# The state-space mixer of a two-block network: gate operands split beside its outputs, second input table loaded by powers, third input product ahead of the first output half

## The chip, the cores and the metric

One core of one Trainium2 chip runs the whole program in one launch. The metric is the device time of one execution in microseconds (us); the median of three runs stands for a kernel. A fourth execution was recorded by the hardware profiler, and all durations below come from that one.

## The reference, cut to what matters

Two networks of depth 2 run one after the other on a sequence of 256 tokens of width 2048. The change touches one mixer, in the second layer of the second network: a state-space layer ("S5") with 128 groups of 16 channels and 64 complex states, cut into chunks of 64 tokens, followed by a gated linear unit:

```python
bu = einsum('bcgi,gpi->bcgp', u_c, b_bar)          # input product
_, states = associative_scan(combine, (a_elem, bu)) # scan along time
y = einsum('bcgp,gip->bcgi', states, c_mat).real    # output product
y = y + d_skip * u
z = gelu(y)
out = z * sigmoid(z @ w_glu + b_glu)                # gate product
```

Before it stands `u = rmsnorm(x) @ odd_w_in`, behind it `out @ odd_w_out`, and then cross-attention and a feed-forward block.

## The kernel before, in words

**Weight products.** Every dense product is a list of tiles ("pieces") of 128 output columns. A tile needs two halves of its weights, a rounded one and the remainder, split from a slab that a DMA brings into a ring of three slabs: ACT rounds all 16 row blocks (L306), DVE makes the remainder of the first eight (L322), POOL that of the last eight (L340). TensorE then runs 16 pairs of matmuls, the pair of L369 (512 columns, both halves of the operand) and L370 (256 columns). The operand itself is also split in two, by ACT (L427, `act_part`) and DVE (L432, `dve_part`), into `opa`, one block of 256 tokens for each of 16 row blocks. The split weights have two buffers in turn, so tile n+2 can be split only when tile n is done. PE, ACT, DVE, POOL and SP each have one instruction list in program order, with semaphore waits; an instruction that waits holds up everything behind it on its engine.

**The mixer.** `pe_odin` makes the 16 tiles of `u` (`K.U`, one row of it per tile). Then the 16 steps n of the scan, four to a stage s (s = 0 to 3), pass through the engines:
- `pe_s5_in(s)` is the input product of four steps, 128 calls of matmul and 256 instructions (L3583), 32 rows by 128 columns of weights from the table `TB[s % 2]` against 64 columns of U. The four row groups of the array take turns, q = 0 to 3. Its results `z5` go to four PSUM banks. The time index r runs over the four powers of the table, power 3 - r being 1024 columns of it.
- `dve_s5` has a body for every n: two products with the rotation table `tab` (L3657, L3664), two additions (L3674, L3675) into step n, and for the step before it the scan (L3671) and the product that makes `p` (L3682), and for the one before that `x` (L3661). ACT copies the scanned state for POOL (`w`, L3638) and makes the tables `tab` (L3545 to L3554), and POOL makes the other half of `p` and `x` (L3712, L3715).
- `pe_s5_out(s, h)` is one half of an output product: 48 instructions of a direct part (L3605) and 128 (L3614) on the p and x of the stage's four steps. `dve_s5_out` (L3697) adds the skip, u5, two rows for each half.
- After all of that ACT applies the gelu to the 16 rows (L3630), then ACT and DVE split them into `opa` (`act_glu`, `dve_glu`), and `pe_glu` runs the gate product: its tile 0 starts at L369 as soon as row block 0 is split.

**The order around the change is written out by hand.** `pe_s5` at L3557 issues in(1); then out(0,0), in(2), out(0,1), out(1,0), in(3), out(1,1), out(2,0), out(2,1), out(3,0), out(3,1). DVE puts the u5 of rows 0, 1 behind step 7, 2, 3 behind step 10, 4, 5 behind 11, 6, 7 behind 14, 8, 9 behind 15, the rest behind step 17. The banks set waits: in(2) may start only when `p` and `w` of step 4 are there, in(3) when those of step 8 are. All output halves but the last use one bank, so each waits for the u5 of the one before. `p5`, eight buffers, lies in a lent ring slab (four) and in the first half of `opa` (four). The p of steps 8 to 11 waits for out(0,1), that of steps 12 to 15 for out(1,1).

**Tables.** `sp_s5_tables` (L3414 on), on SP's queue, loads in this order: TB of stage 1 once tile 14 of `u` is done (`TB[1]` and `TC[1]` lie over the two weight buffers), the c table of stage 1 after tile 15, TB of stage 2 after in(0), the c table of stage 2 after out(0,1), TB of stage 3 after in(1), the c table of stage 3 after out(1,1). TB is loaded by two DMAs (512 KB and 1536 KB, L3375 and L3376), and a c table by one (L3367). The ring slabs lent to the scan are loaded again once the last output half is done.

Of the kernel before, what the change touches and what calls it, by code (L numbers as in the profile page):

```python
# [92 lines left out]
class K:  # L93


    def __init__(self, nc, ctx, D, at, cat):
# [1450 lines left out]
def places2(K):  # L1547
# [2019 lines left out]
def pe_s5_in(K, s):  # L3567

    pe = K.pe
    pe.wait_ge(*K.load[LOADED_B[s]].of(("tb", s)))  # L3570
    pe.wait_ge(*K.dve.of(("u", 4 * s + 3)))
    bs = K.z5b[4 * s:4 * s + 4]
    K.bank.update({("z5", 4 * s + q): bs[q] for q in range(4)})
    if s >= 2:
# [3 lines left out]
    for r in range(4):
        for m in range(4):
            for c in range(2):  # L3580
                for q in range(4):
                    q0 = 32 * q
                    t = pe.do.matmul(bs[q][:, 256 * c + 64 * m:256 * c + 64 * m + 64], B[q0:q0 + 32, 3 - r, m, c, :],  # L3583
                                     K.U[q0:q0 + 32, 4 * s + m, 64 * r:64 * r + 64], start=r + m + c == 0, stop=r + m + c == 7)
# [503 lines left out]
```

## Time and profile before

| what | value |
|---|---|
| median of 3 runs | 4016.72 us (4015.99, 4016.72, 4022.0) |
| profiled execution, own time | 4011.95 us |
| its span in the trace | 4010.6 us |
| mean granted TensorE clock | 0.979 of 2.4 GHz |
| PE busy | 94% of the span |
| DVE, ACT, POOL busy | 64%, 45%, 37% |
| mixer, start of in(1) to start of the gate product's tile 0 | 2867.21 to 2964.36 us |

The page cuts the span in 40 slices of about 100 us. PE is at 90% or more in most of them, and the slice that holds the mixer is one of the few at 80% with a granted clock of 0.8. A row of a timeline gives the start, the duration, the engine, the line, the operation and tiles, and in brackets how long the engine sat idle before it and what ended that. The granted clock is 1.00 at 2.4 GHz and 0.50 at 1.2 GHz.

### The profile page before, as it was taken

Reading aid. Unit: us, or ns where it says so; the run is one execution under the profiler, and the core shown is the slowest. Engines: PE = TensorE matmul, PEld = TensorE weight load, DVE = VectorE, ACT = ScalarE, POOL = GpSimd, SP = SyncE. Lnnn points to the kernel's source line nnn. Section 1 sums busy time; section 2 is a strip of 40 time slices with the busy share of each in tenths; the row PEclk is TensorE's granted clock in tenths of the full one; section 3 lists DMA queues with packets and bytes.
Section 4 is the critical chain, followed back from the end, with each engine's and each line's share of the span. In section 5 each row is a group of like instructions: output and inputs, shape, how many; then the busy total and the mean of one; then the engine's idle time right before and its main releaser. Section 6 shows DMA issues by size and latency. Waiting matters only on the chain.

```text
span 4010.6 us, 64383 instructions
## 1 busy us (share of the span) xinstructions
PE 3781.6 (94%) x27340; PEld 3219.0 (80%) x27340; DVE 2579.5 (64%) x3636; ACT 1799.7 (45%) x2801; POOL 1487.2 (37%) x726
## 2 busy tenths in 40 slices
PE   6898999998998999989999999999879999999998
PEld 3786888787877887888778888888768878888887
DVE  0435743786358897668879676876656776445457
ACT  1435443644345444445544444444445554333334
POOL 0332343233322441004344444444644434444443
PEclk8999999999999999999999999999889999999999
DMA  9653665454643453005355564656445435455553
GB/s 388 271 231 147 235 258 200 161 190 167 247 171 121 171 185 122 23 8 227 139 179 221 199 242 183 227 226 255 162 151 207 168 130 194 181 191 187 189 188 127
DMA packets 60655, 748.64 MB, mean 187 GB/s; under 512 B 6976, under 2 KB 9152, under 8 KB 16720
## 3 DMA queue, kind: packets, MB, share of 16 engines
q1 hardware_dynamic: 48960, 696.74, 45.8%
q0 software_dynamic: 9344, 45.69, 3.0%
q8 instruction: 216, 3.54, 0.4%
q10 hardware_dynamic: 2064, 2.10, 0.1%
q14 instruction: 71, 0.58, 0.0%
HBM read 727.65 MB, written 16.84 MB: 186 GB/s over the span
## 4 chain that ended last, share of the span: by engine, by line
PE 75%; DVE 15%; ACT 5%; DMA 2%; issue 1%; POOL 1%; another core or an unknown queue 0%; SPq 0%; DVEq 0%; ACTq 0%; POOLq 0%
PE ps L369 42%; PE ps L370 21%; DVE pieces L322 3%; DMA ring<-in_ada 2%; ACT pieces L306 2%; PE ps L2228 2%; PE ps L789 2%; DVE opb L570 1%; DVE r L1172 1%; PE ps L3583 1%; DVE opa L570 1%; PE ps L1898 1%; DVE scr L527 1%; DVE scr L591 1%; PE ps L643 1%
## 5 line engine op out<-in xcount | busy, mean ns | idle before, releaser
L369 PE MATMUL ps<-opa,pieces 128*128 128x512 f32 x6192 | 2248.9, 406 | 60.0 <-DVE pieces L322 36.0
L340 POOL TENSOR_TENSOR pieces<-ring,pieces 128x1024 fp32r<-128x1024 f32 x539 | 1348.1, 2501 | 2181.9 <-ACT pieces L306 2163.3
L370 PE MATMUL ps<-opa,pieces 128*128 128x256 f32 x6192 | 1740.6, 281 | 0.0
L306 ACT ACTIVATE pieces<-ring 128x1024 fp32r<-128x1024 f32 (+1 forms) x1110 | 1098.5, 1036 | 807.7 <-PE ps L370 807.0
L369 PEld LDWEIGHTS ps<-opa,pieces 128*128 128x128 f32 x6192 | 1170.9, 189 | 352.6 <-issue 40.1
L370 PEld LDWEIGHTS ps<-opa,pieces 128*128 128x128 f32 x6192 | 1177.7, 190 | 8.9 <-issue 5.3
L369 PE MATMUL ps<-opb,pieces 128*128 128x512 f32 x2560 | 909.1, 396 | 19.4 <-DVE pieces L322 13.7
L322 DVE TENSOR_TENSOR pieces<-ring,pieces 128x1024 fp32r<-128x1024 f32 (+1 forms) x571 | 728.4, 1276 | 269.1 <-ACT pieces L306 265.6
L370 PE MATMUL ps<-opb,pieces 128*128 128x256 f32 x2560 | 725.3, 283 | 0.0
L369 PEld LDWEIGHTS ps<-opb,pieces 128*128 128x128 f32 x2560 | 482.8, 189 | 141.2 <-issue 15.3
L370 PEld LDWEIGHTS ps<-opb,pieces 128*128 128x128 f32 x2560 | 483.4, 189 | 0.1
L427 ACT ACTIVATE opb<-scr 128x256 fp32r<-128x256 f32 x129 | 53.9, 418 | 451.3 <-DVE scr L3072 450.8
L381 DVE TENSOR_REDUCE scr<-ps 128x256 f32<-128x512 f32 x203 | 139.8, 689 | 162.0 <-PE ps L370 161.6
L408 DVE TENSOR_TENSOR x<-ps,x 128x256 f32<-128x256 f32 x192 | 80.8, 421 | 192.5 <-PE ps L370 192.4
L789 PE MATMUL ps<-ring,ada 128*32 128x256 f32 x1536 | 104.5, 418 | 38.1 <-DMA ring<-in_ada 38.1
L527 DVE TENSOR_TENSOR scr<-scr 128x256 f32<-128x256 f32 x165 | 126.3, 783 | 14.5 <-ACT scr L518 11.3
L591 DVE TENSOR_TENSOR scr<-scr,rstd 128x256 f32<-128x256 f32 x136 | 131.1, 964 | 4.6
L789 PEld LDWEIGHTS ps<-ring,ada 128*32 128x32 f32 x1536 | 48.7, 117 | 78.6 <-DMA ring<-in_ada 28.8
L381 DVE TENSOR_REDUCE m<-ps 128x256 f32<-128x512 f32 x48 | 33.2, 691 | 112.1 <-PE ps L370 112.1
L432 DVE TENSOR_TENSOR opb<-scr,opb 128x256 fp32r<-128x256 f32 x129 | 54.8, 425 | 62.5 <-ACT opb L427 62.5
L832 ACT ACTIVATE scr<-ps 128x256 f32<-128x256 f32 x48 | 18.4, 384 | 166.9 <-PE ps L803 148.1
L1063 ACT ACTIVATE scr<-m 128x256 f32<-128x256 f32 x48 | 20.0, 418 | 161.9 <-DVE m L381 161.8
(432 smaller groups left out, 3308.9 us busy)
## 6 DMA issues: line engine op xcount, KB each, us to landing
ring<-in_up SPq DMA_DIRECT2D x64, 2048.0 KB, 7.8
ring<-in_down SPq DMA_DIRECT2D x64, 2048.0 KB, 7.8
ring<-in_win SPq DMA_DIRECT2D x56, 2048.0 KB, 7.6
ring<-in_ada SPq DMA_DIRECT2D x48, 2048.0 KB, 11.9
ring<-in_wout SPq DMA_DIRECT2D x24, 2048.0 KB, 7.6
ring<-in_evin SPq DMA_DIRECT2D x18, 2048.0 KB, 7.8
ring<-in_evout SPq DMA_DIRECT2D x8, 2048.0 KB, 7.8
ring<-in_xkv SPq DMA_DIRECT2D x8, 2048.0 KB, 7.8
```

The source lines that it names most:

```text
L306: a.do.activation(K.parts_of(p)[0][:, s, :], w[:, s, :], ACT.Copy).then_inc(*K.hi.up((p, h)))
L322: v.do.tensor_tensor(lo[:, s, :], w[:, s, :], hi[:, s, :].bitcast(F), ALU.subtract).then_inc(*K.lo.up(p))
L340: g.do.tensor_tensor(lo[:, s, :], w[:, s, :], hi[:, s, :].bitcast(F), ALU.subtract).then_inc(*K.lo2.up(p))
L369: pe.do.matmul(b[:, 0:512], hi[:, k, :], op[:, 512 * k:512 * k + 512], start=i == 0, stop=False)
L370: t = pe.do.matmul(b[:, 0:256], lo[:, k, :], half(op, 0, k), start=False, stop=i == kt - 1)
L381: return K.v.do.tensor_reduce(out, b, AX.X, ALU.add)
L408: v.do.tensor_tensor(x, b[:, 0:256], x, ALU.add).then_inc(*K.dve.up())
L527: v.do.tensor_tensor(K.acc[z], K.acc[z], K.sqr[z][k % 2], ALU.add).then_inc(*K.dve.up((*key, "acc", k)))
L570: K.v.do.scalar_tensor_tensor(out=half(op, 1, k), in0=src, scalar=gain, in1=half(op, 0, k).bitcast(F), op0=ALU.mult, op1=ALU.subtract).the ...
L591: return v.do.tensor_tensor(out, out, rstd[0:out.shape[0]], ALU.mult)
L789: t = pe.do.matmul(b[q:q + 32, 0:256], K.sc[:, 2 * k:2 * k + 32], w[:, k, :], start=k < 4, stop=k >= 12)
L2228: t = K.pe.do.matmul(b[r, 64 * i:64 * i + 64], w[r, i, :], x[r, i, :] if len(x.shape) == 3 else x[r, :], start=start, stop=stop)
```

## The change

The input product of stage 2 moves in front of the first output half, and that of stage 3 in front of out(1,0). The table of stages 1 and 3 is loaded in four DMAs of 512 KB, each with a semaphore of its own, in the order in which the product reads them. The product of stage 1 no longer waits for the last row of u as a whole: the three row groups whose banks are free come first. More output halves have banks of their own. The u5 steps move, the gelu and the first operand splits are put between the last steps, and the p buffers move to the second half of `opa`.

```diff
-    K.p5 = rot(rb, 0, 4, 1024) + rot(f, 8192, 4, 1024)
+    K.p5 = rot(rb, 0, 4, 1024) + rot(f, 12288, 4, 1024)
...
+def load_powers(K, e, s):
+    for k in range(3, -1, -1):
+        src = K.D["s5tb"][s][:, 1024 * k - 1024:1024 * k] if k else K.D["s5b"][s]
+        e.do.dma_start(K.TB[1][:, 1024 * k:1024 * k + 1024], src).then_inc(*K.load["pw%d" % k].up(("tb", s, k), 16))
...
-    load_b(K, sp, 1)
+    load_powers(K, sp, 1)
...
     sp.wait_ge(*K.prod.of(("y5", 3)))
     load_c(K, sp, 2)
     sp.wait_ge(*K.prod.of(("z5", 7)))
-    load_b(K, sp, 3)
+    load_powers(K, sp, 3)
...
 def pe_s5(K):
-    K.pe.wait_ge(*K.dve.of(("u", 15)))
     pe_s5_in(K, 1)
-    for s in range(4):
+    pe_s5_in(K, 2)
+    pe_s5_out(K, 0, 0)
+    pe_s5_out(K, 0, 1)
+    pe_s5_in(K, 3)
+    for s in range(1, 4):
         pe_s5_out(K, s, 0)
-        if s < 2:
-            pe_s5_in(K, s + 2)
         pe_s5_out(K, s, 1)
...
+    rounds = [((0, 1), (0, 1, 2)), ((0, 1), (3,)), ((2, 3), (0, 1, 2, 3))] if s == 1 else [((0, 1, 2, 3), (0, 1, 2, 3))]
+    for powers, rows in rounds:
+        if s == 1 and 3 in rows:
+            pe.wait_ge(*K.dve.of(("u", 15)))
+        for r in powers:
+            if s % 2:
+                pe.wait_ge(*K.load["pw%d" % (3 - r)].of(("tb", s, 3 - r)))
...
+Y5_AT = {(1, 1): 5, (2, 1): 6, (3, 1): 5}
+Y5_AFTER = {(0, 1): 1, (1, 0): 3, (2, 0): 5, (3, 0): 9, (3, 1): 7}
...
+    pe.wait_ge(*K.act.of(("w", {(1, 1): 9, (2, 1): 10}.get((s, h), 0))))
+    if (s, h) in Y5_AFTER:
+        pe.wait_ge(*K.dve.of(("u5", Y5_AFTER[s, h])))
...
-    for n in (13, 14, 15):
-        act_s5_rows(K, n)
-    for i in range(16):
-        a.wait_ge(*K.dve.of(("u5", i)))
-        a.do.activation(K.U[:, i, :], K.U[:, i, :], ACT.Gelu_apprx_tanh).then_inc(*K.act.up(("gelu", i)))
+    a.wait_ge(*K.prod.of(("z5", 15)))
+    act_feed(K, K.first["glu"])
+    act_s5_rows(K, 13)
+    act_s5_gelu(K, 0, 4)
+    act_s5_rows(K, 14)
+    act_s5_gelu(K, 4, 8)
+    act_s5_parts(K, 0, 4)
+    act_s5_rows(K, 15)
+    act_s5_gelu(K, 8, 10)
+    act_s5_parts(K, 4, 8)
+    act_s5_gelu(K, 10, 14)
+    a.wait_ge(*K.prod.of(("y5", 15)))
+    act_s5_parts(K, 8, 14)
+    for i in (14, 15):
+        act_s5_gelu(K, i, i + 1)
+        act_s5_parts(K, i, i + 1)
...
+U5_BEHIND = {7: 0, 10: 2, 13: 4, 14: 6, 16: 8, 17: 10}
...
-    for i in range(10, 16):
+    dve_feed(K, K.first["glu"])
+    for i in range(8):
+        dve_part(K, K.opa, ("gl",), i, K.U[:, i, :])
+    for i in range(12, 16):
         dve_s5_out(K, i)
...
 def dve_glu(K):
     v, p = K.v, K.first["glu"]
-    v.wait_ge(*K.prod.of(("y5", 15)))
-    v.wait_ge(*K.act.of(("gelu", 15)))
-    dve_feed(K, p)
-    for i in range(16):
+    for i in range(8, 16):
         dve_part(K, K.opa, ("gl",), i, K.U[:, i, :])
```

`act_s5_gelu` and `act_s5_parts` are the old loops over gelu and `act_part`, cut to a range of rows. `U5_BEHIND[n]` names the first of the two rows of u5 put behind step n. U rows 12 to 15 stand behind the splits of rows 0 to 7. `Y5_AT` gives the bank and `Y5_AFTER` the row of u5 that an output half waits for. The first six lines of `act_glu` (feed and 16 splits) are gone.

## Rows read from the trace of the kernel before

**Rows 1.** Timeline of PE: start, duration, engine, line, operation, count, idle before.

```profile
2839.82 7.37 PE L3583 MATMUL ps<-s5u 32*128 32x64 f32 x256
...
2867.21 11.90 PE L3583 MATMUL ps<-s5u,s 32*128 32x64 f32 x256 [2.54 <-DVE ps L3671]
...
2886.32 3.60 PE L3614 MATMUL ps<-ring,mix 128*32 128x63 f32 x128 [4.49 <-DVE ps L3674]
...
2897.18 1.51 PE L3605 MATMUL ps<-s5u,scr 32*32 32x192 f32 x48
2898.63 1.97 PE L3614 MATMUL ps<-ring,mix 128*32 128x63 f32 x128
2910.10 2.78 PE L3605 MATMUL ps<-s5u,scr 32*32 32x192 f32 x48 [9.50 <-DVE s5u L3697]
...
2915.24 8.01 PE L3583 MATMUL ps<-s5u,s 32*128 32x64 f32 x256
...
2957.72 0.32 PE L3614 MATMUL ps<-s 128*32 128x64 f32 x7 [1.61 <-issue]
2964.36 0.76 PE L369 MATMUL ps<-opa,pieces 128*128 128x512 f32 x1 [6.32 <-DVE opa L432]
```

**Rows 2.** Timeline of DVE, same columns.

```profile
2879.17 0.69 DVE L3657 TENSOR_TENSOR ring<-ps,ring 128x512 f32<-128x512 f32 x1 [2.83 <-PE ps L3583]
...
2895.04 0.86 DVE L3697 SCALAR_TENSOR_TENSOR s5u<-s5u,cols,ps 128x256 f32<-128x256 f32 x2
2897.33 0.69 DVE L3657 TENSOR_TENSOR ring<-ps,ring 128x512 f32<-128x512 f32 x1 [1.42 <-PE ps L3583]
...
2923.30 0.69 DVE L3657 TENSOR_TENSOR ring<-ps,ring 128x512 f32<-128x512 f32 x1 [7.07 <-PE ps L3583]
...
2944.82 0.69 DVE L3682 TENSOR_TENSOR s<-ps,s5u 128x512 f32<-128x512 f32 x1
...
2961.65 7.59 DVE L432 TENSOR_TENSOR opa<-s5u,opa 128x256 fp32r<-128x256 f32 x16
...
2972.07 0.69 DVE L381 TENSOR_REDUCE mix<-ps 128x256 f32<-128x512 f32 x1 [1.70 <-PE ps L370]
...
2977.62 0.69 DVE L381 TENSOR_REDUCE mix<-ps 128x256 f32<-128x512 f32 x1 [2.04 <-PE ps L370]
```

**Rows 3.** Timeline of ACT: the end of table 4, and the copy w of step 4.

```profile
2876.50 0.40 ACT L3554 ACTIVATE ring<-scr 128x256 f32<-128x256 f32 x1
...
2887.27 0.60 ACT L3638 ACTIVATE scr<-ps 128x512 f32<-128x512 f32 x1 [1.24 <-DVE s L3682]
```

**Rows 4.** Windows: PE, PEld, DVE, ACT, POOL busy (x instructions), granted clock, DMA, GB/s.

```profile
2867.20:2879.10 11.90, 11.89 (x260) 11.78 (x264) 9.13 (x20) 8.07 (x21) 9.25 (x8) 0.60 0.77 325
...
2886.30:2889.90 3.60, 3.58 (x132) 3.43 (x132) 3.60 (x9) 2.57 (x8) 3.02 (x3) 0.50 0.02 5
...
2900.60:2910.10 9.50, 0.00 (x1) 0.01 (x1) 9.50 (x21) 6.41 (x16) 7.99 (x7) 0.66 0.89 347
...
2915.30:2923.20 7.90, 7.85 (x260) 7.56 (x259) 0.87 (x2) 2.71 (x8) 4.76 (x4) 1.00 0.02 4
```

**Rows 5.** DMA issues from 2858 to 2880 us: tiles, size, us to landing.

```profile
s<-in_s5b SPq DMA_DIRECT2D x1, 512.0 KB, 3.2
```

**Rows 6.** DMA issues from 2900 to 2916 us, all behind the end of out(0,1).

```profile
s<-s_b_tables SPq DMA_DIRECT2D x1, 1536.0 KB, 11.9
s<-in_s5b SPq DMA_DIRECT2D x1, 512.0 KB, 8.7
```

**Rows 7.** Line L3583: its instructions, duration in ns min/median/max.

```profile
L3583 PEld LDWEIGHTS ps<-s5u x512: 181/187/217, 2839.8 to 2896.9; 32*128 32x128 f32 x171
L3583 PE MATMUL ps<-s5u x512: 270/270/354, 2839.8 to 2897.0; 32*128 32x64 f32 x171
```

**Rows 8.** Timeline of POOL: the split of the last eight blocks of tile 0.

```profile
2961.48 2.45 POOL L340 TENSOR_TENSOR pieces<-ring,pieces 128x1024 fp32r<-128x1024 f32 x1 [13.15 <-ACT pieces L306]
```

**Rows 9.** DMA issues from 2957 to 2985 us.

```profile
ring<-in_glu SPq DMA_DIRECT2D x4, 2048.0 KB, 7.8
```

More of the change, by code:

```diff
@@ L3569, in pe_s5_in @@
     pe = K.pe
-    pe.wait_ge(*K.load[LOADED_B[s]].of(("tb", s)))
-    pe.wait_ge(*K.dve.of(("u", 4 * s + 3)))
     bs = K.z5b[4 * s:4 * s + 4]
     K.bank.update({("z5", 4 * s + q): bs[q] for q in range(4)})
+    pe.wait_ge(*K.dve.of(("u", 4 * s + 3) if s == 0 else ("u", 14)))
     if s >= 2:
@@ L3576, in pe_s5_in @@
         pe.wait_ge(*K.act.of(("w", 4 * s - 4)))
+    if s % 2 == 0:
+        pe.wait_ge(*K.load["tb%d" % s].of(("tb", s)))
     B = K.TB[s % 2].rearrange("p (k m c t) -> p k m c t", k=4, m=4, c=2)
[L3578 to L3584, printed above, removed]
+    rounds = [((0, 1), (0, 1, 2)), ((0, 1), (3,)), ((2, 3), (0, 1, 2, 3))] if s == 1 else [((0, 1, 2, 3), (0, 1, 2, 3))]
[5 more added lines that the diff above has]
+                pe.wait_ge(*K.load["pw%d" % (3 - r)].of(("tb", s, 3 - r)))
+            for m in range(4):
+                for c in range(2):
+                    for q in rows:
+                        q0 = 32 * q
+                        t = pe.do.matmul(bs[q][:, 256 * c + 64 * m:256 * c + 64 * m + 64], B[q0:q0 + 32, 3 - r, m, c, :],
+                                         K.U[q0:q0 + 32, 4 * s + m, 64 * r:64 * r + 64], start=r + m + c == 0, stop=r + m + c == 7)
     t.then_inc(*K.prod.up(("z5", 4 * s + 3)))
+Y5_AT = {(1, 1): 5, (2, 1): 6, (3, 1): 5}
+Y5_AFTER = {(0, 1): 1, (1, 0): 3, (2, 0): 5, (3, 0): 9, (3, 1): 7}
 def pe_s5_out(K, s, h):
     pe = K.pe
-    b = K.bank["y5", s, h] = K.ps[5] if (s, h) == (3, 1) else K.ps[3]
+    b = K.bank["y5", s, h] = K.ps[Y5_AT.get((s, h), 3)]
     pe.wait_ge(*K.act.of(("K", 0)))
-    pe.wait_ge(*K.act.of(("w", 12 if (s, h) == (3, 1) else 0)))
-    if s + h and (s, h) != (3, 1):
-        pe.wait_ge(*K.dve.of(("u5", 4 * s + 2 * h - 1)))
+    pe.wait_ge(*K.act.of(("w", {(1, 1): 9, (2, 1): 10}.get((s, h), 0))))
+    if (s, h) in Y5_AFTER:
+        pe.wait_ge(*K.dve.of(("u5", Y5_AFTER[s, h])))
     if s:
@@ L3625, in act_s5, with act_s5_gelu, act_s5_parts @@
             act_s5_whole(K, n // 2 + 1)
-    for n in (13, 14, 15):
-        act_s5_rows(K, n)
-    for i in range(16):
-        a.wait_ge(*K.dve.of(("u5", i)))
-        a.do.activation(K.U[:, i, :], K.U[:, i, :], ACT.Gelu_apprx_tanh).then_inc(*K.act.up(("gelu", i)))
+    a.wait_ge(*K.prod.of(("z5", 15)))
[14 more added lines that the diff above has]
+        act_s5_parts(K, i, i + 1)
+def act_s5_gelu(K, i, j):
+    for i in range(i, j):
+        K.a.wait_ge(*K.dve.of(("u5", i)))
+        K.a.do.activation(K.U[:, i, :], K.U[:, i, :], ACT.Gelu_apprx_tanh).then_inc(*K.act.up(("gelu", i)))
+def act_s5_parts(K, i, j):
+    K.a.wait_ge(*K.tile.of(K.first["odin"] + 15))
+    for i in range(i, j):
+        K.a.wait_ge(*K.act.of(("gelu", i)))
+        act_part(K, K.opa, ("gl",), i, K.U[:, i, :])
 def act_s5_rows(K, n):
```

24 lines of the change are left out of this document (7 added, 17 removed).

## The prediction

> **What bounds the kernel now.** The page comes first: PE is busy nearly everywhere, so only the places where it stands still can give something back, and the slice with the mixer is one of them. Then the timelines of PE and DVE side by side. In the mixer the two hand the work to and fro. PE stands 4.49 us before the second part of out(0,0) and 9.50 us before out(1,0); DVE starts step 4 only with the end of in(1), after 2.83 us idle, step 8 with the end of in(2) after 1.42, and step 12 with the end of in(3) after 7.07 [rows 1, 2]. Then comes the tail: the last output half ends at 2958.04, and PE waits 6.32 us until a first row of `opa` is split, at 2964.36; tile 0 is done at 2972.07 [rows 1, 2]. So what counts is which of the four input products DVE waits for, and the tail. Last the windows, for TensorE's clock: it is at 1.00 in the one product in(3) and at 0.60 over in(1) [rows 4].
>
> From the end of tile 0 on nothing is changed and PE is the bound (tiles end 5.55 us apart, at 2972.07 and 2977.62 [rows 2]), so the shift of that end is the shift of the whole. I follow the change from in(1) to it, in times of the old trace.
>
> **in(1).** Its last table quarter came with a whole 1536 KB load; now the first quarter is 512 KB, and such a load alone took 3.2 us [rows 5], so it is there before tile 15 ends (about 2864.7, 2.54 us before 2867.21 [rows 1]). The product starts at 2864.7 without a pause. Its rounds: 96 instructions on three row groups, 32 on one, 128 on four. The normal spacing is 7.37/256 = 0.029 us [rows 1]. For the 32 on one row group there is no row. Bounds: 0.029 each (0.9 us), or load and matmul one after the other, 187 + 270 = 457 ns [rows 7], 14.6 us. I take 0.06 (1.9 us), twice the spacing of the nearest row, which is in(0) [rows 1], since weight load and matmul of different instructions plainly overlap there. Sum 2.8 + 1.9 + 3.7 = 8.4, end 2873.1; with the high value 2885.8. DVE needs it for step 4, but also `tab` of step 4, whose last instruction ends at 2876.90 [rows 3] and hangs on POOL's angles, which don't move. So step 4 starts at 2876.9, 2.3 us earlier, and in(1) has 3.8 us to spare, up to 0.18 us for each of the 32. By the Trainium skill, "TensorE: Matmul & The Clock Gate", section Part 3, a weight load overlaps running matmuls only when its row group differs. By that rule the loads of the single group alone, 32 x 187 ns, would take 6.0 us, in(1) would end at 2877.2, and step 4 would lose 0.3 us; no row here shows such a round. Four DMA issues for two on SP's queue cost some 0.9 us of its time, hidden: what is queued behind them (c table 1, table 2) is wanted only after 2885.
>
> **in(2), moved ahead.** It waits for w of step 4. That ended 8.70 us after step 4 began (2887.87 less 2879.17 [rows 2, 3]); so now at 2885.6. PE has then stood since 2873. At which clock does it run? In the old trace the clock is down after pauses (0.50 with out(0,0) after 4.49 us idle, 0.66 over 9.5 us of nothing [rows 1, 4]), and in(1) itself ran 11.9 us at a mean of 0.60 without coming back: 7.37/0.60 = 12.3, so these 32-row matmuls did not lift it, while the 128-row matmuls of L3614 did (0.50 at 2886.3, then in(2) at full speed in front of L3605's 1.51 us) [rows 1, 4]. in(3) ran in 8.01 at 1.00 because it followed out(1,0). So I take a cold in(2): twice the 7.37 less what is fixed, 14.0 us, against 7.4 warm. It ends at 2899.6, and the old one ended at 2897.18 [rows 1].
>
> **out(0,0), now behind it, and who waits.** Direct part cold 2.78, L3614 between 1.97 and 3.60, say 2.8 [rows 1]: it ends at 2905.2. In DVE's list u5 of rows 0, 1 stands behind step 7 and in front of step 8, and needs this half. DVE is through step 7 at 2892.8 (its end moved by 2.3 from 2895.04 [rows 2]) and stands 12.4 us. After 0.86 for u5 [rows 2] step 8 starts at 2906.1: **8.8 us later** than 2897.33.
>
> **Steps 8 to 11, out(0,1), in(3).** out(0,1) runs warm 1.51 + 1.97 less overlap = 3.4, ends 2909.5. SP has the c table of stage 2 in front of the quarters, and both behind this end: the first 512 KB after such an end landed 8.7 us after an issue 0.4 us behind it, the rest of the table 11.9 after its own [rows 6]. So in(3) starts at about 2918.6, after 9 us idle, cold, 14.0 us, end 2932.6. DVE would be ready at 2906.1 + 4 x 3.97 + 0.8 = 2922.8 (a step is (2895.04 - 2879.17)/4 = 3.97 [rows 2]), so in(3) decides again. Step 12 starts **9.3 us later** than 2923.30.
>
> **Steps 12 to 17.** out(1,0) 5.6 (2.78 + 2.8) to 2938.2, out(1,1), in its own bank, 3.4 to 2941.6. The p of step 12, due at 2939.9, waits for it: 1.7 us lost. Then u5 of 4, 5, steps 14 and 15 with u5 of 6, 7 to 2951.8, step 16 without its products 2.4 (to 2954.2), u5 of 8, 9 to 2955.0. Here out(2,0) and out(2,1) lie beside the steps. out(3,0), waiting for that u5, starts 2955.0 at the low clock, 5.6, and out(3,1) 3.4: end at **2964.0**. Old: from step 12 at 2923.30 to 2958.04 34.7 us, new 31.4, so 3.3 saved, since DVE no longer feeds the halves one by one. The old p of step 15 came at 2944.82 [rows 2], and then PE worked off three halves.
>
> **The tail.** Gelu, tile 0's split by ACT and DVE, and the splits of rows 0 to 7 lie beside steps 14 to 17 and out(3,0). The split of eight rows on DVE costs at most 7.59/2 = 3.8 us [rows 2]; behind 2955.8 it is over at 2961, before y of out(3,0) is wanted by u5 of 12, 13. If that cover is gone it costs these 3.8. At 2964.0 PE starts tile 0 at once, warm. POOL's remainder for blocks 8 to 15 needs 2.45 [rows 8], PE comes to block 8 after 2.8 us, half of 5.55. The eight late rows on DVE come 0.41 apart and tile 0 takes them at 0.35, which adds 0.2. End of tile 0 at 2969.8: 5.8 us behind the last half where it was 14.0, **8.2 saved**. The next slab is issued with the end of out(3,1) and lands 7.8 later [rows 9], 2971.8; with 2.3 us of splits 2974.1, tile 2 is due at 2975.4: hidden, with 1.3 to spare.
>
> **Sum.** +9.3 - 3.3 - 8.2 = -2.2 us. Profiled execution 4011.95 - 2.2 = 4009.8; the median of the runs is 4.8 above that execution, so 4016.72 - 2.2 = **4014.5 us**. A difference of 0.2% (8 us) is about what a measurement can tell from none.
>
> **Rivals.**
> - *B, in(2) is warm.* Then 7.4 us, end 2893.0, out(0,0) 3.5, step 8 at 2897.4, as before; in(3) still late by its table and cold, step 12 at 2923.9. Sum +0.6 - 3.3 - 8.2 = -10.9: 4005.8. For it: in(0) and in(3) ran at full clock. Against it: 9.8 us of cold in(1) with no rise. The Trainium skill ("TensorE: Matmul & The Clock Gate", Part 1) has the clock released by sustained activity, which would lift in(2) in its course; in(1)'s row speaks against it for this form. Chance 0.2, with mixtures.
> - *C, the single row group.* From 0.18 us for each of the 32, in(1) becomes late. At 0.457 and a low clock in its last round (7.0) it ends at 2889, 12 us behind 2876.9, and steps 4 on with it: -2.2 + 12 = +10: 4026.5. For it: nothing in the trace runs on one row group alone with so few columns. Against: the tight spacing of in(0), 0.029 us where a load lasts 0.187 [rows 1, 7]. Chance 0.08.
> - *D, the cover in the tail fails*: the eight early splits stand in front of the last u5, PE waits their 3.8 us, and the stall of 1.61 us on issue before the last seven matmuls [rows 1] returns. -2.2 + 3.8 + 1.6 = +3.2: 4019.9. Chance 0.12.
> - *E, the change doesn't do what it says*: the two moved products save no wait, since DVE stands for out(0,0) and in(3) for its table, and the splits are waited for as before. Then the losses of 9.3 stand against 3.3 alone: +6, 4022.7. The wait on `opa` is gone by the code, so I give it no chance of its own; it is in C's.
>
> **How the numbers follow.** The forecast has 0.6, with a range of its own of 4009.5 to 4019 (each of three clock changes may fall 1.5 us earlier or later). To hold 8 in 10 the range goes down to B, 4005, and up to D, 4020.5. Faster by over 0.2% is B: 0.2. Slower by over 0.2% is C and a little of D: 0.1. Same 0.7.
>
> **What would show it.** Right: L3583 starts at 2864.7 with no idle time; DVE's L3697 for rows 0 and 1 has over 10 us idle before it, released by L3614; in(2) lasts near 14 us at 0.5; in(3) starts 9 us behind the end of out(0,1); PE's idle time before the first L369 of the gate product is gone. Wrong: step 8 of DVE starts before 2900, or in(2) lasts under 9 us (B); step 4 starts after 2878 (C); a pause over 2 us before tile 0 (D).

## The result and the profile after

The changed kernel runs in 4018.88 us (median of 20 runs, 4016.77 to 4027.71), the kernel before in 4014.89 us (20 runs, 4005.71 to 4026.82). The ratio is 1.0014, with a 95% interval of 1.0007 to 1.0020: **5.6 us slower**, 2.8 to 8.0 (the medians alone are 4.0 apart). Forecast were 2.2 us less; 4018.88 lies inside the range given, but the sign is the other one. The profiled execution of the changed kernel took 4020.42 us (span 4019.1, mean granted clock 0.978) where that of before took 4011.95, so the two traces differ by 8.5 us. Of these, 1.3 us lie ahead of the mixer: tile 15 of u ends at 2865.94 and not at 2864.67.

The timeline of PE after the change (start, duration, engine, line, operation, tiles, count, idle before and its releaser; L3594 is the old L3583, L3620 the old L3605, L3629 the old L3614):

```profile
2865.66 0.28 PE L370 MATMUL ps<-opa,pieces 128*128 128x256 f32 x1
2865.87 15.27 PE L3594 MATMUL ps<-s5u,s 32*128 32x64 f32 x256
2889.96 13.93 PE L3594 MATMUL ps<-s5u 32*128 32x64 f32 x256 [8.82 <-DVE ring L3701]
2903.82 2.78 PE L3620 MATMUL ps<-s5u,scr 32*32 32x192 f32 x48
2906.53 2.96 PE L3629 MATMUL ps<-ring,mix 128*32 128x63 f32 x128
...
2923.20 13.93 PE L3594 MATMUL ps<-s5u,s 32*128 32x64 f32 x256 [9.28 <-DVE s5u L3741]
...
2954.80 1.18 PE L3620 MATMUL ps<-s5u,scr 32*32 32x128 f32 x38 [3.47 <-issue]
...
2963.73 1.97 PE L3629 MATMUL ps<-s 128*32 128x63 f32 x128 [2.02 <-POOL s L3759]
...
2967.79 0.31 PE L3620 MATMUL ps<-s5u,scr 32*32 32x64 f32 x7 [0.72 <-issue]
...
2971.26 0.32 PE L3629 MATMUL ps<-s 128*32 128x64 f32 x7 [1.33 <-issue]
2971.51 0.50 PE L369 MATMUL ps<-opa,pieces 128*128 128x512 f32 x1
```

Against [rows 1]: in(1) starts without a pause, but lasts 15.27 us where the old one took 11.90 and the forecast was 8.4. in(2) and in(3) are both 13.93 us long, where the old trace had 7.4 and 8.01. A product that runs at 1.2 GHz is called cold below, one at 2.4 GHz warm. in(3) itself waits for no u5 (L3741) in the program; run 11 has the load of its table at this place, and run 7 tests it. In the last line the gate product follows the last output half at once; the 6.32 us of waiting in [rows 1] are gone.

The timeline of DVE, same columns (L3701 is the old L3657, L3741 the old L3697):

```profile
2881.18 0.69 DVE L3701 TENSOR_TENSOR ring<-ps,ring 128x512 f32<-128x512 f32 x1 [3.57 <-PE ps L3594]
...
2909.57 0.87 DVE L3741 SCALAR_TENSOR_TENSOR s5u<-s5u,cols,ps 128x256 f32<-128x256 f32 x2 [12.45 <-PE ps L3629]
2910.36 0.68 DVE L3701 TENSOR_TENSOR ring<-ps,ring 128x512 f32<-128x512 f32 x1
...
2937.18 0.69 DVE L3701 TENSOR_TENSOR ring<-ps,ring 128x512 f32<-128x512 f32 x1 [9.36 <-PE ps L3594]
...
2962.93 3.29 DVE L432 TENSOR_TENSOR opa<-s5u,opa 128x256 fp32r<-128x256 f32 x8
...
2977.78 0.67 DVE L381 TENSOR_REDUCE mix<-ps 128x256 f32<-128x512 f32 x1
```

The four L3701 and L3741 rows are the starts of step 4, of u5 for rows 0 and 1, and of steps 8 and 12. The 12.45 us in front of u5 are the stand that was forecast (12.4). The last row starts 0.20 us behind the end of tile 0 on PE (2977.58), from which the times below are taken.

The windows of the same trace (us, then PE, PEld, DVE, ACT, POOL busy (x instructions), granted clock, DMA share, GB/s):

```profile
2869.40:2870.90 1.50, 1.50 (x24) 1.50 (x21) 1.50 (x4) 1.15 (x3) 0.47 (x1) 1.00 1.07 459
2870.90:2889.90 19.00, 10.24 (x146) 10.05 (x145) 15.43 (x32) 11.12 (x30) 15.66 (x14) 0.51 0.36 149
2889.90:2903.80 13.90, 13.84 (x256) 13.77 (x256) 7.22 (x15) 8.34 (x22) 12.81 (x11) 0.50 0.01 3
2903.80:2908.50 4.70, 4.70 (x128) 3.92 (x128) 0.00 (x0) 0.00 (x0) 0.00 (x0) 0.50 0.00 0
```

The clock falls at 2871.1, inside in(1), and is at its lower level for 37.5 us, through all of in(2) and most of out(0,0). In the third row PE is busy the whole time and the clock doesn't move.

Step by step, in us behind the end of tile 15 of each trace:

| point | before | forecast | after | after less forecast |
|---|---|---|---|---|
| in(1) ends | 14.4 | 8.4 | 15.2 | +6.8 |
| step 4 starts | 14.5 | 12.2 | 15.2 | +3.0 |
| in(2) | 25.2 to 32.6 | 20.9 to 34.9 | 24.0 to 37.9 | +3.0 |
| step 8 starts | 32.7 | 41.4 | 44.4 | +3.0 |
| in(3) | 50.6 to 58.6 | 53.9 to 67.9 | 57.3 to 71.2 | +3.3 |
| out(3,0) starts | 83.3 | 90.3 | 94.3 | +4.0 |
| last half ends | 93.4 | 99.3 | 105.6 | +6.3 |
| tile 0 ends | 107.4 | 105.1 | 111.6 | +6.5 |
| tile 15 ends | 190.6 | | 197.0 | |

So the miss at tile 0 is 3.0 us from in(1), 0.3 on the way to in(3), 3.0 within the output halves and 0.2 behind them. The next 15 tiles add 2.2 us that the forecast had at nothing, and what comes behind tile 15 the last 0.7 of the 8.5.

### The profile page after: what moved, and what is told of

The parts are those of the page before. It is cut to its first block, busy times and chain, and to the rows that moved or that the text cites. A ratio compares the mean times of both kernels' runs of the same rounds, so it can differ in the third digit from the quotient of the medians.

```text
span 4019.1 us, 64388 instructions
## 1 busy us (share of the span) xinstructions
PE 3796.4 (94%) x27340; PEld 3230.7 (80%) x27340; DVE 2575.8 (64%) x3636; ACT 1798.9 (45%) x2801; POOL 1481.9 (37%) x726
## 4 chain that ended last, share of the span: by engine, by line
PE 77%; DVE 14%; ACT 5%; DMA 2%; issue 1%; POOL 1%; another core or an unknown queue 0%; SPq 0%; DVEq 0%; ACTq 0%; POOLq 0%
PE ps L369 43%; PE ps L370 22%; DVE pieces L322 2%; DMA ring<-in_ada 2%; ACT pieces L306 2%; PE ps L2228 2%; PE ps L789 2%; PE ps L3594 1%; DVE r L1172 1%; PE ps L1898 1%; DVE opa L570 1%; DVE scr L591 1%; PE ps L643 1%; PE ps L1043 1%; DVE opb L570 1%
## 5 line engine op out<-in xcount | busy, mean ns | idle before, releaser
L322 DVE TENSOR_TENSOR pieces<-ring,pieces 128x1024 fp32r<-128x1024 f32 (+1 forms) x571 | 721.5, 1264 | 268.5 <-ACT pieces L306 265.1
L369 PEld LDWEIGHTS ps<-opb,pieces 128*128 128x128 f32 x2560 | 482.7, 189 | 141.0 <-issue 15.3
L427 ACT ACTIVATE opb<-scr 128x256 fp32r<-128x256 f32 x129 | 53.9, 418 | 451.0 <-DVE scr L3072 450.5
L527 DVE TENSOR_TENSOR scr<-scr 128x256 f32<-128x256 f32 x165 | 126.2, 782 | 14.5 <-ACT scr L518 11.3
```

Source lines behind the costliest of these rows:

```text
L322: v.do.tensor_tensor(lo[:, s, :], w[:, s, :], hi[:, s, :].bitcast(F), ALU.subtract).then_inc(*K.lo.up(p))
L369: pe.do.matmul(b[:, 0:512], hi[:, k, :], op[:, 512 * k:512 * k + 512], start=i == 0, stop=False)
L527: v.do.tensor_tensor(K.acc[z], K.acc[z], K.sqr[z][k % 2], ALU.add).then_inc(*K.dve.up((*key, "acc", k)))
```

## The experiments

The letters in the expectations: **R**, the rounds of in(1) cost time; **O**, the place of in(2) does; **C**, the clock is what makes in(2) and in(3) long; **T**, step 12 hangs on in(3) and its table and not on step 8; **L**, the profile of before shows an execution with an early rise of the clock. "Tile 0" below is its end behind the end of tile 15 of u, as in the table.

**1. in(1) in one round.**

```diff
-    rounds = [((0, 1), (0, 1, 2)), ((0, 1), (3,)), ((2, 3), (0, 1, 2, 3))] if s == 1 else [((0, 1, 2, 3), (0, 1, 2, 3))]
+    rounds = [((0, 1, 2, 3), (0, 1, 2, 3))]
```

> The changed kernel with in(1) in one round of four row groups, power by power, waiting for the last row of u; all else kept. In the changed kernel in(1) took 15.27 us: 3.6 for the 96 on three row groups, 3.9 for the 32 on one, the rest at the low clock, and step 4 of DVE began 15.2 us behind the end of tile 15 (14.5 before the change). Theory R (the rounds are the loss): in(1) takes 8 to 13 us, step 4 begins 12.3 to 14 us behind tile 15, and all that follows moves with it, 1.5 to 3 us less for the kernel. Rival P (the quarters of the table arrive too late for any order): step 4 stays at 15 us or later, no gain.

Measured: ratio to before 1.0005 (0.9996 to 1.0014). in(1) 12.02 us, 3.2 less than with rounds, though it starts 1.5 later behind the last row of u; step 4 at 13.5 (15.2), tile 0 at 110.2 (111.6). The rounds cost 1.7 us at step 4, at the low end of R: in(1) in one round is still long, since the clock falls 2.1 us after its start all the same (0.58 mean). in(2) and in(3) stay at 13.93. The ratio was 1.0014 with the rounds, so 3.6 us less by the runs, which were measured at another time than those of the changed kernel.

**2. in(2) back behind out(0,0).**

```diff
-    pe_s5_in(K, 2)
     pe_s5_out(K, 0, 0)
+    pe_s5_in(K, 2)
```

> The changed kernel with in(2) put back behind out(0,0); in(3) stays ahead of out(1,0). Theory O (the order of in(2) is the loss: it runs at the low clock after a pause, and DVE stands for out(0,0) behind it): in(2) takes 7.4 us instead of 13.9, DVE's idle time of 12.45 us before u5 of rows 0 and 1 is gone, step 8 begins 34 to 35 us behind tile 15 instead of 44.4, and the kernel is 8 to 11 us faster than the changed one, so 3 to 6 us faster than the kernel before. Rival W (step 12 waits for the table of stage 3 and for the clock whatever happens before): step 8 gains 10 us, step 12 under 4 us, the kernel under 4 us.

Measured: 0.9996 (0.9985 to 1.0006). PE's timeline of this kernel:

```profile
2865.21 15.24 PE L3594 MATMUL ps<-s5u,s 32*128 32x64 f32 x256
...
2891.11 7.37 PE L3594 MATMUL ps<-s5u 32*128 32x64 f32 x256
...
2911.37 13.93 PE L3594 MATMUL ps<-s5u,s 32*128 32x64 f32 x256 [9.54 <-DVE s5u L3741]
```

in(1) is as long as in the changed kernel and in(2) is warm again. Step 8 starts at 33.3 (44.4), tile 0 ends at 100.8 (111.6). The sign is that of O, but not all of the 10.9 us belongs to the order. In this order in(2) was cold in two other traces (runs 3 and 9), and there step 8 starts at 39.9: at the same clock the place of in(2) is worth 4.5 us at step 8, and the other 6.6 are the clock. By the runs the kernel is 1.6 us faster than before (6.0 faster to 2.4 slower), where 3 to 6 were expected.

**3. The old order and loads, the new tail alone.** The moves of in(2) and in(3), the rounds and the loads by powers are undone; the u5 places, the banks, the gelu and the early splits stay.

```diff
-    for k in range(3, -1, -1):
...
+    e.do.dma_start(K.TB[1][:, 0:1024], K.D["s5b"][s]).then_inc(*K.load["pw0"].up(("tb", s, 0), 16))
+    e.do.dma_start(K.TB[1][:, 1024:4096], K.D["s5tb"][s]).then_inc(*K.load["pw1"].up(("tb", s, 1), 16))
...
-    pe_s5_in(K, 2)
-    pe_s5_out(K, 0, 0)
-    pe_s5_out(K, 0, 1)
-    pe_s5_in(K, 3)
-    for s in range(1, 4):
+    for s in range(4):
         pe_s5_out(K, s, 0)
+        if s < 2:
+            pe_s5_in(K, s + 2)
...
```

> Tail alone: the changed kernel with the order of products, the single round and the two-part table loads of before; what stays is the gelu and the splits between the steps, the u5 places, the banks and the place of the p buffers. Both products warm as before, steps 8 and 12 at 32.7 and 58.6 us behind tile 15 as before. Theory: the last half ends about 92 us behind tile 15 and tile 0 of the gate product 6 us after it, so 8 to 10 us less than before the change (0.2 to 0.25%). Rival S (the stalls on issue in the output halves, 7.3 us in the changed kernel against 3.0 before, belong to the tail part of the change): the last half ends at 95 or later, and the gain is 3 to 5 us.

Measured: 0.9989 (0.9980 to 0.9998), so 4.4 us faster where 8 to 10 were expected. In the profile tile 0 ends at 105.1, only 2.3 before that of the kernel before, although 6.0 us lie between the last half and tile 0 (14.0 before). The trace shows why: in(2) took 13.93 us here, in the very order in which the old timeline has it at 7.4. The row of this run, and that of the kernel before:

```profile
2891.68 13.93 PE L3592 MATMUL ps<-s5u 32*128 32x64 f32 x256
...
2889.86 7.40 PE L3583 MATMUL ps<-s5u 32*128 32x64 f32 x256
```

This run made L: two executions with the same instructions in this place are not in the same clock. Runs 9 and 10 test it.

**4. The clock held up in front of in(2).** 22 matmuls whose result nothing reads, on 128 rows and 512 columns; nothing else differs.

```diff
     pe_s5_in(K, 1)
+    K.pe.wait_ge(*K.act.of(("w", 0)))
+    for _ in range(22):
+        K.pe.do.matmul(K.ps[3][:, 0:512], K.opa[:, 0:128], K.opa[:, 0:512], start=True, stop=True)
     pe_s5_in(K, 2)
```

> The changed kernel with 22 extra matmuls of 128 rows by 512 columns, whose result nobody reads, between in(1) and in(2), in the pause of 8.82 us. Theory C (the cold in(2) is the clock's doing and not a property of the product): the granted clock is 1.00 when in(2) begins, in(2) takes 7.4 to 8.5 us instead of 13.93, out(0,0) 3.5 instead of 5.7, and step 8 begins 7 to 9 us earlier than in the changed kernel. Rival: in(2) takes over 12 us (32-row matmuls with no clock above the low one after a pause), no gain or a loss by what the extra work adds. For the kernel: the gain carries over to step 12 if the table of stage 3, ordered at the end of out(0,1), moves with it: 6 to 9 us less.

Measured: 1.0001 (0.9991 to 1.0012). PE's timeline, and the windows of all engines:

```profile
2866.10 15.92 PE L3597 MATMUL ps<-s5u,s 32*128 32x64 f32 x256
2881.95 7.95 PE L3564 MATMUL ps<-opa 128*128 128x512 f32 x22
2890.76 7.37 PE L3597 MATMUL ps<-s5u 32*128 32x64 f32 x256 [0.87 <-DVE ring L3704]
```

```profile
2884.00:2886.00 2.00, 2.00 (x7) 1.52 (x6) 2.00 (x5) 0.00 (x0) 0.45 (x1) 0.50 0.00 0
2886.00:2888.00 2.00, 2.00 (x7) 1.57 (x6) 2.00 (x5) 1.84 (x5) 1.20 (x1) 0.58 0.00 0
2888.00:2890.70 2.70, 1.89 (x9) 1.23 (x7) 2.70 (x7) 1.44 (x5) 2.17 (x3) 1.00 0.00 0
...
2890.70:2898.10 7.40, 7.33 (x260) 7.30 (x261) 7.23 (x15) 4.91 (x14) 6.65 (x6) 1.00 0.02 4
```

The clock rises while the added matmuls run, near 2888. At 1.00 in(2) takes 7.37 us; tile 0 ends at 105.1, 6.5 before that of the changed kernel. Order, rounds and waits are the changed kernel's, so the long in(2) is the clock's doing: C holds. in(3), with no such work in front, is cold again (14.23). Expected were 6 to 9 us less for the kernel than changed; the runs give 1.0001 beside 1.0014 of the changed kernel, so 5 less, again from runs at another time.

**5. The rounds in in(0) too**, one execution.

```diff
-    rounds = [((0, 1), (0, 1, 2)), ((0, 1), (3,)), ((2, 3), (0, 1, 2, 3))] if s == 1 else [((0, 1, 2, 3), (0, 1, 2, 3))]
+    rounds = [((0, 1), (0, 1, 2)), ((0, 1), (3,)), ((2, 3), (0, 1, 2, 3))] if s < 2 else [((0, 1, 2, 3), (0, 1, 2, 3))]
```

> The cost of the rounds by itself: the changed kernel with in(0), which runs in the middle of full-speed tiles, cut into the same three rounds as in(1). In the changed kernel in(0) takes 7.37 us. Inside in(1) the 96 on three row groups went 37 ns apart, the 32 on one at 112 ns while the clock was still full, then up to 175. Theory G (single row group: load and matmul of neighbours no longer overlap): in(0) takes 96 x 0.037 + 32 x 0.112 + 128 x 0.029 = 10.9 us at full clock. Rival K (the clock's fall made the round slow, not the row group): in(0) takes 7.4 to 8.5 us. Between the two lies the case that the clock falls during the round, then 12 to 15 us.

Measured: 4032.59 us in its one execution. in(0) stands amid the tiles of u, all its data there, at full clock. The timeline and the windows of this line alone:

```profile
2845.91 15.27 PE L3594 MATMUL ps<-s5u 32*128 32x64 f32 x256
```

```profile
2845.90:2849.40 3.50, 3.49 (x96) 3.49 (x99) 1.00 0.00 0
2849.40:2853.30 3.90, 3.90 (x38) 3.90 (x34) 0.73 0.02 4
2853.30:2861.00 7.70, 7.70 (x133) 7.69 (x133) 0.50 0.01 2
```

in(0) takes 15.27 us where [rows 1] has 7.37. The three windows are the three rounds. The starts of the single instructions in the trace show how they go. In each turn the matmuls of the different row groups start together, 6 to 7 ns apart, and the next turn follows 112 ns later at the full clock and 213 ns later at the low one, whether one, three or four groups take part. That is 112 ns for each instruction on one group, 37 on three and, in in(0) as it was, 29 on four; at the low clock 213 on one and 53.4 on four. So the instruction count is not the cost, but the turns: 96/3 + 32 + 128/4 = 96 of them in rounds, 64 in one round of four groups. In(1) of the changed kernel has the same paces, in its windows of this line:

```profile
2865.90:2869.40 3.50, 3.50 (x99) 3.50 (x100) 1.00 0.95 309
2869.40:2873.30 3.90, 3.90 (x40) 3.90 (x36) 0.72 0.99 417
2873.30:2880.80 7.50, 7.50 (x133) 7.50 (x132) 0.50 0.61 253
```

The round on one group takes 4.1 us for 32 instructions (from 2869.38 to 2873.47 in the changed kernel). In run 5 the clock comes down within it, 5.25 us after the start of in(0), with no wait and hardly a transfer about (DMA share 0.00 to 0.02); in the other 13 traces in(0) has no rounds and keeps 1.00 to its end. It is the case between the two theories (12 to 15 us): G's price for the rounds, 32 turns more, and the clock's fall on top. That the rounds bring the clock down is shown in this one execution alone, and for in(0) alone; in(1) loses it without rounds too (run 1).

**6. The u5 of rows 0, 1 behind step 8**, one execution.

```diff
-U5_BEHIND = {7: 0, 10: 2, 13: 4, 14: 6, 16: 8, 17: 10}
+U5_BEHIND = {8: 0, 10: 2, 13: 4, 14: 6, 16: 8, 17: 10}
```

> The changed kernel with u5 of rows 0 and 1 put behind step 8 instead of step 7, so that step 8 of DVE needs in(2) alone. Step 8 begins at 38 us behind tile 15 instead of 44.4. Theory T (in(3) waits for its table, which is loaded behind out(0,1), and step 12 for in(3)): out(0,1), the table, in(3) and step 12 stay where they are, 48, 57, 71 us, and the kernel gains nothing. Rival D (DVE's chain of steps sets the end): step 12 begins 4 to 6 us earlier and the kernel gains as much.

Measured: 4021.24 us. Step 8 starts at 40.3 (44.4), but in(3) at 59.2 (57.3) and step 12 at 73.2 (71.2): DVE's stand moves from u5 to step 12, where it idles 12.98 us. in(1) ended 1.6 us later in this execution, which is most of the 2.0 at step 12. T: nothing gained.

**7. The powers of stage 3 in front of the c table of stage 2**, one execution.

```diff
-    sp.wait_ge(*K.prod.of(("y5", 3)))
-    load_c(K, sp, 2)
     sp.wait_ge(*K.prod.of(("z5", 7)))
     load_powers(K, sp, 3)
+    sp.wait_ge(*K.prod.of(("y5", 3)))
+    load_c(K, sp, 2)
```

> The changed kernel with the quarters of the stage 3 table ordered ahead of the wait for out(0,1) and of the c table of stage 2. They land long before 45 us behind tile 15. in(3) then waits only for w of step 8, about 53 us, instead of 57.2 us. Theory T: in(3) begins 4 us earlier, at the low clock again (5 us pause), 13.9 us long, step 12 at 67 instead of 71.2, the last half and the gate product 4 us earlier. Rival (issue stalls and POOL's last x decide the end): step 12 gains 4 us, the gate product under 2.

Measured: 4011.03 us. in(3), in PE's timeline of this kernel:

```profile
2916.82 13.93 PE L3594 MATMUL ps<-s5u,s 32*128 32x64 f32 x256 [5.15 <-DVE ring L3701]
```

Its idle time falls from 9.28 to 5.15 us and its releaser is now DVE's step 8. Step 12 starts at 67.1 (71.2), tile 0 ends at 107.1 (111.6). T again: the table was what held in(3).

**8. All together:** one round, in(2) behind out(0,0), powers first, and in the tail ACT's tables of step 15 before the splits of rows 0 to 3 and DVE's weight split of the gate product behind its eight operand splits.

```diff
-    act_s5_parts(K, 0, 4)
     act_s5_rows(K, 15)
+    act_s5_parts(K, 0, 4)
...
-    dve_feed(K, K.first["glu"])
     for i in range(8):
         dve_part(K, K.opa, ("gl",), i, K.U[:, i, :])
+    dve_feed(K, K.first["glu"])
```

> All repairs together: in(1) in one round, in(2) behind out(0,0), the stage 3 quarters ahead of out(0,1), and in the tail ACT's copy of step 15 ahead of the splits of rows 0 to 3 and DVE's split of tile 0 behind the eight splits. Expected: step 4 at 13.5 us behind tile 15, step 8 at 31 to 35, in(3) begins at w of step 8, about 41, and lasts 8 (full clock) to 14 us, step 12 at 50 to 55 instead of 71, the last half at 84 to 89, tile 0 of the gate product ends at 90 to 95 where it ended at 107.4 before the change and 111.6 after. Kernel 12 to 17 us (0.3 to 0.4%) faster than before. Rival: stalls on issue in the output halves grow as PE has fewer pauses to fetch in, and half of it is lost.

Measured: 0.9975 (0.9964 to 0.9986), median 4003.48 us: 10 us faster than the kernel before, where 12 to 17 were expected. PE's timeline:

```profile
2871.81 7.36 PE L3594 MATMUL ps<-s5u,s 32*128 32x64 f32 x252 [1.46 <-DVE s5u L401]
2881.50 0.44 PE L3594 MATMUL ps<-s5u,s 32*128 32x64 f32 x4 [2.33 <-issue]
...
2951.66 1.97 PE L3629 MATMUL ps<-s 128*32 128x63 f32 x128 [0.93 <-POOL s L3759]
```

Step 8 starts at 32.2, step 12 at 55.1, the last half ends at 89.7, tile 0 at 95.7. The wait for POOL's x in the last halves is 0.93 us instead of 2.02. in(3) is still cold, 13.93 us. in(1), the same single round as in run 1, ran warm to its end here (7.36 us before its stall, 12.02 in run 1): its clock too differs from execution to execution.

**9. The kernel before, profiled again.**

> The kernel before, profiled once more, nothing changed. In its first profile in(1), in(2), in(3) took 11.9, 7.4 and 8.0 us, and DVE's steps 8 and 12 began 32.7 and 58.6 us behind the end of tile 15. Theory L (at which clock a product runs depends on where the clock's changes fall, which is another place in each execution): one or more of the three products has another length, by 1 to 6.5 us, and step 12 begins anywhere between 57 and 66. Rival (fixed by the program): the same lengths within 0.3 us.

Measured: 4028.94 us. PE's timeline of this second execution:

```profile
2874.61 12.54 PE L3583 MATMUL ps<-s5u,s 32*128 32x64 f32 x256 [2.49 <-DMA s<-s_b_tables]
...
2894.48 3.60 PE L3614 MATMUL ps<-ring,mix 128*32 128x63 f32 x128 [4.63 <-DVE ps L3674]
2898.01 13.93 PE L3583 MATMUL ps<-s5u 32*128 32x64 f32 x256
...
2931.82 7.37 PE L3583 MATMUL ps<-s5u,s 32*128 32x64 f32 x256 [0.41 <-DMA s<-s_b_tables]
```

```profile
2889.70:2898.00 8.30, 3.67 (x136) 3.39 (x128) 8.30 (x17) 5.15 (x14) 5.87 (x6) 0.71 0.01 2
2898.00:2911.90 13.90, 13.90 (x264) 13.77 (x260) 6.07 (x14) 6.48 (x17) 10.99 (x10) 0.50 0.01 3
```

The same code, and in(2) takes 13.93 us and not 7.4. The clock came back for a part of the first window and was down again before in(2); in [rows 4] it was up just ahead of it. Tile 0 ends at 117.2 and not at 107.4. L holds: the trace on which the forecast rests was the better of the two by 9.8 us in this stretch. But 4028.94 is also more than any of the 77 timed executions of this kernel (4005.06 to 4027.35), so this second trace is an extreme one and not the usual case.

**10. The new tail alone, once more, with more rounds.** The kernel of run 3.

> The tail alone, the kernel of e3_old_order once more. There in(2) took 13.93 us against 7.4 in the profile of before, though the work ahead of it is the same, and the gain at tile 0 was 2.3 us instead of 8 to 10. Theory L (that was the place of the clock's changes): with in(2) at full speed the last half ends at 92 to 94 and tile 0 at 98 to 100 us behind tile 15. If in(2) is cold again: 105 as in the first look. The timed runs average over it: 4 to 9 us faster than before.

Measured: 0.9967 (0.9955 to 0.9979), median 4004.12 us. Here in(2) took 7.53 us and tile 0 ended at 97.9. The four traces pair up: warm against warm, the tail saves 107.4 - 97.9 = 9.4 us, cold against cold 117.2 - 105.1 = 12.1. By the ratio it is 13.3 us, more than the 4 to 9 expected and three times the 4.4 of run 3, with the same kernel. The two went to different chips, their intervals just fail to meet, and the kernel before had a median of 4013.51 us beside run 3 and of 4017.22 beside run 10. So one ratio can be some 9 us off the next, beyond its own interval, and only kernels that were measured together are set side by side below.

**11. The changed kernel, profiled again.**

> The changed kernel, profiled once more. in(2) follows a pause of over 8 us and a stretch at the low clock: theory L says that it and in(3) are cold in each execution (13.9 us both), as in e1, e5, e6 and e7, so the changed kernel has lost a lottery that the kernel before wins at times; only in(1) may vary, 15 to 17 us. Tile 0 of the gate product ends 110 to 114 us behind tile 15. Rival: in(2) or in(3) under 12 us.

Measured: 4015.87 us. in(1) 15.38, in(2) and in(3) 13.93 each, step 12 at 71.3, tile 0 at 111.5: within 0.2 us of the first trace. In all six traces with in(2) in front of out(0,0) and no added matmuls (the two of the changed kernel, runs 1, 5, 6 and 7) in(2) and in(3) take 13.93 us; behind out(0,0) in(2) took 7.4 to 8.0 in five traces and 13.93 in two. In the changed kernel the slow clock is no matter of luck, and that fits the runs: before spreads over 21 us, after lies within 6 us in 19 of 20.

**12. Run 8 with the clock held up before in(1) and in(3)** by 6 and 22 such unread matmuls.

```diff
+def pe_busy(K, bank, n):
+    for _ in range(n):
+        K.pe.do.matmul(bank[:, 0:512], K.opa[:, 0:128], K.opa[:, 0:512], start=True, stop=True)
...
+    pe_busy(K, K.z5b[4], 6)
     pe_s5_in(K, 1)
...
+    K.pe.wait_ge(*K.dve.of(("p", 5)))
+    K.pe.wait_ge(*K.act.of(("w", 5)))
+    pe_busy(K, K.z5b[12], 22)
     pe_s5_in(K, 3)
```

> e8_all with extra matmuls of 128 rows by 512 columns that nobody reads: 6 in front of in(1) (pause 1.46 us) and 22 between out(0,1) and in(3) (pause 5.6 us). Theory C (the low clock behind a pause is what makes the products slow): in(1) takes 7.4 to 8 us in every execution, in(3) 7.4 to 8 us instead of 13.93, step 12 begins at 49 to 50 us behind tile 15 instead of 55, bound by DVE's own steps, and the kernel is 4 to 6 us faster than e8_all. Rival: in(3) is no faster, or step 12 begins at 54 or later since the extra matmuls hold it up; no gain.

Measured: 0.9950 (0.9937 to 0.9964), median 3998.52 us against 4017.22 of before and 4004.12 of run 10, measured together, with no overlap with the latter's runs (3996.50 to 4001.51; 4003.43 to 4008.56). It is the **best version** here. PE's timeline:

```profile
2870.20 1.55 PE L3562 MATMUL ps<-opa 128*128 128x512 f32 x6
2871.84 7.14 PE L3603 MATMUL ps<-s5u,s 32*128 32x64 f32 x246
2880.23 0.55 PE L3603 MATMUL ps<-s5u,s 32*128 32x64 f32 x10 [1.25 <-issue]
2894.58 7.58 PE L3603 MATMUL ps<-s5u 32*128 32x64 f32 x256
2905.44 5.29 PE L3562 MATMUL ps<-opa 128*128 128x512 f32 x22
2911.50 7.51 PE L3603 MATMUL ps<-s5u,s 32*128 32x64 f32 x255 [0.78 <-DVE ring L3710]
```

All three input products run at the full clock but for the first 0.5 us of in(2). Step 12 starts at 49.8 (55.1 in run 8), tile 0 ends at 89.8 (95.7). The gain is in(3), 7.51 us instead of 13.93: the 22 matmuls fill the wait in which the clock fell in run 8. What the 6 in front of in(1) bring is not shown, since in(1) was warm in run 8 without them. Run 8 was not measured beside this one; the 5.9 us between their traces fit the 4 to 6 expected.

## Why the prediction was wrong, point by point

- **in(1): the step that failed.** "Sum 2.8 + 1.9 + 3.7 = 8.4" was 3.5 + 4.1 + 7.7 = 15.3 us. Two things were wrong in it. The pace: "I take 0.06", for which no row was at hand, was 0.112 us, since a turn takes as long with one row group as with four (run 5). And the clock: all three terms were taken at 2.4 GHz, though [rows 4] have in(1) of the kernel before at a mean of 0.60 and the next paragraph of the prediction builds on that. An estimate from the turns tells the two apart: 96 turns of 0.112 us are 10.8 us, which is still in front of the 12.2 at which step 4's table is ready, so the rounds alone would have been hidden (in run 8, where in(1) ended at 11.6, step 4 starts at 12.3, released by ACT's table). The fall of the clock, in the middle of the second round, adds the other 4.5. Of the 6.8 us too many the slack of 3.8 took its share, and 3.0 came through to step 4. Run 1 agrees: in one round, with the clock falling in it too, step 4 is at 13.5, 1.3 behind the forecast.
  Rival C had the place and the direction right, and its sign came (step 4 at 2879.9 in times of the old trace, "after 2878"). It named 0.18 us for each of the 32 as the point where in(1) gets late; they took 0.128 on the mean, so its low clock in the last round was needed too. Its own price of 457 ns was more than twice too high. The table loads that ran beside in(1) (309 and 417 GB/s) are not needed for it: run 5 has next to none and the same 15.27. By the Trainium skill, "TensorE: Matmul & The Clock Gate", section Part 3, a weight load overlaps running matmuls only when its row group differs. This case's trace does not bear that out: on the one group of run 5 each load (187 ns) starts 56 ns behind the start of the matmul ahead of it, the next matmul follows another 56 ns later, and the turn is no longer than with four groups. The measurement decides.
- **in(2): right.** 14.0 forecast, 13.93 measured; the clock stayed low for its whole length (0.50). Rival B falls, and what made it fall is shown by run 4: 22 matmuls on 128 rows in front of it and it takes 7.37. By the Trainium skill, "TensorE: Matmul & The Clock Gate", section Part 1, sustained activity releases the clock. The trace does not agree for this form: these 256 matmuls on 32 rows, back to back for 13.9 us, stayed at 0.50 to their end, while in run 4 the clock rose within 7.95 us of matmuls on 128 rows.
- **Who waits for out(0,0): right.** DVE stood 12.45 us, forecast 12.4. Run 2 has tile 0 10.9 us earlier without the move; 4.5 of that is the order at the same clock, the rest a warm in(2).
- **in(3) and its table: right.** 9.28 us idle (9 forecast), 13.93 us long, and it decides step 12 (runs 6 and 7).
- **The output halves: 3.0 us too short, the second step that failed.** out(3,0) started 0.7 us later still. It took 5.5 us as forecast (5.6), but not for the reason given: it ran warm, and 2.02 of it were a wait for POOL's x, a queue that the step left out. out(3,1) took 5.9 and not 3.4: PE stood 0.72 and 1.33 us on issue. The sum had this at nothing without a reason, and kept it for rival D, though the kernel before stands 1.61 us there [rows 1] and 0.96 a little earlier. D's cause, eight splits in front of the last u5, did not come: they ran from 2962.93 for 3.29 us beside the halves, and no PE wait names them.
- **The tail: right.** 6.0 us from the last half to the end of tile 0, forecast 5.8, before 14.0.
- **From tile 0 on "nothing is changed": not so.** Tile 1 took 6.25 us. In all 12 traces with the new tail it takes 6.15 to 6.29, in the two of the kernel before 5.55 and 5.66, so some 0.6 us is a price of the change: in the changed kernel PE stands 0.32 us at its start for DVE's weight split (L322), which comes behind the eight late operand splits. The rest is the spacing: tiles 3 to 15 lay 5.65 apart in this trace and 5.55 in the second (67.84 and 66.56 us for twelve), and in the kernel before it was 5.55 in the first and 5.65 in the second. So that differs from execution to execution, and is worth 1.5 us over 14 tiles. Why was not tried.
- **The base: an error not seen in the sum.** All was set against one execution in which in(2) was warm. Against the cold one of run 9 the changed kernel's tile 0 ends 5.6 us earlier, against the warm one 4.3 later. How often each comes is not measured; the runs mix them, and gave 5.6 us slower.

In the sum the tail saved about what it should (9.4 and 12.1 us for the 3.3 + 8.2 = 11.5 forecast). What was put in front of it, the moves, rounds and loads, lost 13.7 us against the warm trace of the tail alone (111.6 against 97.9) and 6.5 against its cold one (105.1).

## What to carry to other kernels

A product of small matmuls, moved out of the cover of larger ones, can cost twice its time by the clock alone; look at what PE did before it, and weigh a few large unread matmuls in a wait that PE has anyway (run 12). Keep all row groups filled in each turn: a round that leaves one group alone, to start on work 1.5 us earlier, took 4.1 us for 32 instructions, which four groups do in 0.9 (8 turns of 112 ns). Count turns and not instructions. Where a stage runs near a change of clock, take a second profile of the same kernel before sizing a step of a few us. And where the kernel before stands on issue, keep that wait in the sum unless something takes it away.

## What the runs showed of the hardware

- Matmuls of 32 rows and 64 columns on different row groups start together, 6 to 7 ns apart, and a turn takes 112 ns at 2.4 GHz and 213 at 1.2 with one, three or four groups (run 5, the changed kernel). So four groups do four times the work of one in the same time, also with only 64 columns.
- The clock fell within a round on one row group amid dense work (run 5, from 1.00 to 0.50, one execution), and 2.1 us into a product on four groups behind a pause of 1.46 us (run 1); the same product ran warm to its end in run 8.
- The same program can have the clock rise in one place in one execution and a few microseconds away in the next; for in(2) that is 7.4 or 13.9 us (runs 3, 9, 10 and the profile of before).
- PE stands "on issue" 0.2 to 3.5 us in dense runs of small matmuls: 2.33 us before the last four of in(1) in run 8, 1.25 before the last ten in run 12. The places are fixed by the program: within one trace these stalls are a multiple of 128 matmuls apart, or one or two off it (255, 128, 255 and 128 in both traces of the changed kernel), which with their weight loads is a multiple of 256 instructions. The profile of the changed kernel has a DMA queue for instructions (packets, MB, share of 16 engines), so its packets are 16 KB each:

```profile
q8 instruction: 216, 3.54, 0.4%
```

  In the changed kernel four of its packets end at 2953.47, 2957.40, 2966.29 and 2969.81, and the stalls of 3.47, 1.40, 0.72 and 1.33 us end at 2954.80, 2958.82, 2967.79 and 2971.26. In all 14 traces the 58 stalls of 0.2 us and more in this stretch end 1.2 to 1.6 us behind such a packet. So PE waits there for its own instructions, as far as times can tell; no run changed the loading of instructions to test it.
